# The order behind the state steps of a two-layer hybrid trunk, its last residual sum on two engines, and one weight split behind an eviction

## The chip, the cores and the metric

The kernel runs on one core of a Trainium2 chip. The core has TensorE for matrix products, VectorE, ScalarE and GpSimd for work on elements, and SyncE (SP), which here only issues transfers. Every engine works through a queue of its own, in order, and waits on semaphores that the others raise. The metric is the device time of one execution in microseconds, lower is better.

## What is computed

A trunk of two layers on 256 tokens of width 1024, float32. Each layer is, cut to what matters here:

```
u = rms_norm(x)
q, k, v, z, a, b, cq, ckv, k_rope, gates = split(u @ W_in)
# branch A: short causal conv and SiLU on q, k, v; l2 norm of q and k; gated delta rule in chunks
o_a = gated_delta_rule(q, k, v, g, beta)          # per head, a triangular solve and a state step
y_a = (rms_norm(o_a) * silu(z)) @ W_a
# branch B: latent attention with rotary keys
q_b = rms_norm(cq) @ W_uq ; k_b, v_b = rms_norm(ckv) @ W_ukv ; k_pe = rope(k_rope)
y_b = softmax(q_b k_b^T + mask) v_b @ W_b
h = sigmoid(g_A) * y_a + sigmoid(g_B) * y_b ;  x = x + rms_norm(h @ W_out)
x = x + rms_norm(relu(rms_norm(x) @ W1)^2 @ W2)
```

## The kernel before

Everything is held transposed, features on the 128 partitions and the 256 tokens along the free dimension, so a tile of two feature chunks is 128x512. A dense product is made of three products of split operands: each operand is a high part (`whi`, `uh`, `xh`) in a short format and a low part (`wlo`, `ul`, `xl`), and TensorE computes hi x hi, lo x hi and hi x lo into one of three PSUM banks `dense`. The weights come as 152 pieces a layer of 128x1024 through a ring of four buffers: SP loads `raw`, ScalarE copies it to `whi` (`split_hi`), VectorE subtracts to get `wlo` (`split_lo`), TensorE uses both. SP may load a piece when the `wlo` of the piece four before is made; ScalarE may write `whi` when TensorE is through with the piece four before.

One list, `ORDER`, is written out by the function `schedule`, and each engine walks it once per layer and takes from each entry what is its own. So `ORDER` sets the queue of every engine. An entry `("job", j)` is a dense product of 256 output features with its eviction, `("half", j)` the first half of one. Ahead of an entry stand the splits of the pieces that `splits_wanted` gives it: a job asks for the splits up to four pieces ahead of its last one. The kinds of job are: `lat` (the latents; the third, `lat` 2, also holds the rotary key and the logits a and b, which VectorE puts into `krx`), `k`, `z`, `v`, `q`, `gate`, `kn` and `vt` (keys and values of branch B), `uq` (its queries), `ya`, `yb`, `out`, `ff1` and `ff2`.

The small steps that the text speaks of are entries too. `t_v0`, `t_st`, `t_ks` and `t_v1` are the state steps of the delta rule between its two chunks, with VectorE's `vn` and `rr`; `qk` is the product of keys and queries (L888) with VectorE's decay of it into `DT` (L1667); `t_o` forms the output `oT` from 24 small products (L1009 to L1011), and ScalarE evicts it. `q2` is a square of `qT` on ScalarE (L1270), which enters the norm of the output. That norm has for each of four pairs of heads: `osq`, ScalarE's square of `oT` (L1276) and GpSimd's addition of `q2` to it (L1914), into one of two buffers `sq`; `onrm`, TensorE's sum over the partitions (L1020), ScalarE's logarithm and exponential (L1120, L1122) and VectorE's scaling of `oT` (L1718); `osplit`, GpSimd's product with `zs` (L1920) and the split into `oh` and `ol`. `osq` of pair 2 or 3 waits until the sum of the pair two before has left the buffer. `kr` is the rotary turn of the shared key: one product (L856) and VectorE's block of seven operations from `krb` to `krz`; `qrope` is the same for the queries. `lnexp` loads a table of functions on ScalarE. `sc`, `tr` and `pv` are the attention: scores, the softmax on VectorE (L1733 to L1743), transposes (L1056), values. `logits` starts with a product of `krx` (L787).

At the end of a layer `post` scales `yT` by `rn` (`times_norm`, L1810) and adds it to `xT` (`add`, L1815) on VectorE; in the last layer SP stores `xT` in four pairs of chunks as they come.

Of the kernel before, what the change touches and what calls it, by code (L numbers as in the profile page):

```python
# [19 lines left out]
ALU = mybir.AluOpType  # L20
# [4 lines left out]
DEPTH, D, S = 2, 1024, 256  # L25
# [18 lines left out]
RING = 4  # L44
# [42 lines left out]
JOBS, NPIECE = jobs_of_a_layer()  # L87
JOB = {(kind, i): j for j, (kind, i, _) in enumerate(JOBS)}
# [4 lines left out]
NDVE_EVAC = NJOB - NACT_EVAC  # L93
# [17 lines left out]
def evacs_through(j):  # L111

    mine = JOBS[j][0] in EVAC_BY_ACT
    return mine, sum((k in EVAC_BY_ACT) == mine for k, _, _ in JOBS[:j + 1])
# [5 lines left out]
def schedule():  # L120
# [4 lines left out]
    def job(kind, i, after=None):  # L125
        o.append(("job", JOB[kind, i]))
        flush()
        if after:
            late.append((after, i))
# [47 lines left out]
    behind = {n: [] for n in range(len(shares))}  # L177
# [8 lines left out]
    behind[3].append(("trig", 0))  # L186
    for n, at_ in enumerate((7, 9, 10, 13)):
        behind[at_].insert(0, ("vtrans", n))
    for n, at_ in enumerate((1, 3)):
        behind[at_].insert(0, ("ktrans", n))  # L190
    steps = [[(step, lv)] for lv in range(len(SIZES)) for step in ("lvP", "lvV")]
# [3 lines left out]
    for n, share in enumerate(shares):  # L195
# [11 lines left out]
            o.extend(ready[at_unit])  # L207
            at_unit += 1
        o.extend(behind[n])
    o.append(("q2", 0))  # L210
    job("vt", 0)
    o += [("qk", 0), ("qk", 1), ("qd", 0), ("kr", 0)]
    job("vt", 1)
    o += [("q2", 1), ("q2", 2), ("q2", 3), ("lnexp", 1), ("t_o", 0)]
    job("vt", 2)
    o += [("qk", 2), ("qk", 3), ("qd", 1)]
    job("vt", 3)
    for n, i in enumerate((4, 5, 0, 1, 2, 3)):
        job("uq", i)
        if i >= 4:  # L220
            late.append(("qrope", i - 4))
        if n == 0:
            o.append(("t_o", 1))
        if n >= 2:
            o.append(("onrm", n - 2))
        if 1 <= n < 5:
            o.append(("osq", n - 1))
    o += [("exptanh", 0), ("sc", 0), ("osplit", 0), ("osplit", 1)]
    for n in range(6):
        job("gate", 1 + n)  # L230
# [47 lines left out]
def build(nc, x_in, pos_in, w_in, prm_in, cst_in, out):  # L278
    with ExitStack() as ctx:
# [17 lines left out]
        xT = keep("xT", [P, KD, S])  # L297
# [107 lines left out]
        def over_heads(ap, n):  # L405

            return ap.rearrange("p (a w) -> p a w", a=1).broadcast_to([P, n, ap.shape[1]])
# [84 lines left out]
        def due(l, s, n):  # L492

            return l * rises_per_layer[s.name] + n
# [24 lines left out]

        def splits_wanted(l, what, n):  # L520

            if what == "job":
                return min(l * NPIECE + JOBS[n][2][-1] + RING, DEPTH * NPIECE)
            if what == "half":
                return l * NPIECE + JOBS[n][2][0] + RING
            if what == "ahead":
                return min(l * NPIECE + (NPIECE if n else JOBS[JOB["ff1", 0]][2][0]) + RING, DEPTH * NPIECE)
            if what == "u":
                return l * NPIECE + (8 if n >= 2 else 0)
            if l:  # L530
                return l * NPIECE + (4 if (what, n) == ("xsplit", 1) else 0)
            return {("xsplit", 1): 1, ("xsplit", 2): 2, ("sq", 0): 3, ("sqsum", 1): 4}.get((what, n), 0)
# [13 lines left out]
        @block.sync  # L546
        def _(sp):
            def x_part(c):
                sp.dma_start(xT[:, 2 * c:2 * c + 2, :], x_in[:, 2 * c:2 * c + 2, :]).then_inc(s_x[c], 16)

            for n in range(DEPTH * NPIECE):
                if n == 2:
                    x_part(2)
                    x_part(3)
                elif n < 2:
                    x_part(n)
                sp.wait_ge(lo_ready, n + 1)
                sp.dma_start(raw[n % RING][:], w_in[n]).then_inc(loaded[n % RING], 16)
                if n == RING - 1:
                    sp.dma_start(cst[:, 0:C_FREQ], cst_in[:, 0:C_FREQ]).then_inc(s_in, 16)  # L560
                    sp.dma_start(pos_i[:], pos_in).then_inc(s_tab, 16)
                    sp.dma_start(cst[:, C_FREQ:NCST], cst_in[:, C_FREQ:NCST]).then_inc(s_tab, 16)
            for c in range(4):
                pair = slice(2 * c, 2 * c + 2)
                sp.wait_ge(x_done, due(DEPTH, x_done, 2 * c + 2))
                sp.dma_start(out[:, pair, :], xT[:, pair, :]).then_inc(s_out, 16)
            sp.wait_ge(s_out, 4 * 16)

# [862 lines left out]
        def _(dve):  # L1431
# [373 lines left out]
            def post(l, n):  # L1805
                w, part = divmod(n, 2)

                def times_norm(c0, c1):
                    cs = slice(c0, c1)
                    TT(yT[:, cs, :], yT[:, cs, :], over_heads(rn[0][:, 0:S], c1 - c0), ALU.mult).then_inc(y_scaled, c1 - c0)  # L1810
# [6 lines left out]
                def low(e):  # L1817
# [6 lines left out]
                    elif l + 1 < DEPTH:  # L1824
                        x_low(l + 1, e)

                if part:
                    low(6)
                    low(7)
                    return  # L1830
                dve.wait_ge(y_r, due(l, y_r, 2 * w + 2))
                dve.wait_ge(dve_evac, l * NDVE_EVAC + evacs_through(JOB["ff2" if w else "out", 3])[1])
                times_norm(0, 1)
                add(0, 1)
                times_norm(1, 2)
# [39 lines left out]
        def _(pool):  # L1875
# [47 lines left out]
                pool.wait_ge(dve_evac, l * NDVE_EVAC + evacs_through(JOB["ff1", i])[1])  # L1923
                G(fr[i % 4][:], fr[i % 4][:], fr[i % 4][:], ALU.mult).then_inc(f_sq, 1)  # L1924

            do = dict(squares=squares, yadd=yadd, qd=qd_, zero=zero, osq=osq, osplit=osplit, fsplit=fsplit)
            pool.wait_ge(s_in, 16)
            for l in range(DEPTH):
                for what, n in ORDER:
# [115 lines left out]
```

## Time and profile before

| | us |
|---|---|
| median of 3 runs | 1043.33 (1041.62 to 1043.66) |
| profiled execution | 1044.15 |
| its span | 1042.4 |
| TensorE busy | 1013.2 (97%) |
| VectorE busy | 727.2 (70%) |
| ScalarE busy | 559.0 (54%) |
| GpSimd busy | 96.4 (9%) |

The span runs from the first to the last instruction of one execution; the profiled execution took 1.75 us more. Busy shares are of the span. The granted clock of TensorE was 0.993 of full speed over the span. In the names of the profile PE is TensorE, DVE is VectorE, ACT is ScalarE, POOL is GpSimd, and SPq is SP's queue of transfers; L1020 is line 1020 of the kernel.

### The profile page before, as it was taken

How to read it: one execution, taken by the hardware profiler on the slowest of the kernel's cores; microseconds unless marked ns; L12 is line 12 of the kernel's file. 1: busy time of each engine (PE TensorE's matmuls, PEld its weight loads, DVE VectorE, ACT ScalarE, POOL GpSimd, SP SyncE). 2: the span in 40 equal slices, each digit the busy share in tenths (PEclk: the TensorE clock that was granted, in tenths of full speed). 3: DMA queues.
4: the chain of work that ended last, by engine and by line, in shares of the span. 5: the costliest groups of instructions: out<-in, count | busy, mean ns of one | idle time of the engine just before them, and what ended most of it. 6: DMA issues, size and time to landing. Idle time of an engine off the chain costs nothing.

```text
span 1042.4 us, 24322 instructions
## 1 busy us (share of the span) xinstructions
PE 1013.2 (97%) x10626; PEld 984.9 (94%) x10626; DVE 727.2 (70%) x1024; ACT 559.0 (54%) x791; POOL 96.4 (9%) x76
## 2 busy tenths in 40 slices
PE   9999999899999999999999999998999999999996
PEld 8999899799999999999999999997999999999995
DVE  7887766588566788644598667656865777885543
ACT  7665684645445645444466645756554445544441
POOL 0010000120000222100000100004000003221000
PEclk9999999999999999999999989999999999999998
DMA  8544433424565466666635344333255646666661
GB/s 294 163 130 136 145 105 120 120 75 169 177 190 181 135 200 193 202 198 188 181 105 179 122 127 146 119 104 120 84 180 182 186 139 190 195 191 198 198 182 41
DMA packets 45609, 163.86 MB, mean 157 GB/s; under 512 B 5184, under 2 KB 5440, under 8 KB 45504
## 3 DMA queue, kind: packets, MB, share of 16 engines
q1 hardware_dynamic: 45360, 162.16, 50.2%
q8 instruction: 84, 1.38, 0.5%
q14 instruction: 21, 0.17, 0.1%
q10 hardware_dynamic: 144, 0.15, 0.0%
HBM read 161.25 MB, written 1.05 MB: 156 GB/s over the span
## 4 chain that ended last, share of the span: by engine, by line
PE 82%; issue 8%; DVE 7%; ACT 2%; POOL 1%; DMA 0%; SPq 0%; DVEq 0%; POOLq 0%; ACTq 0%
PE dense L613 22%; PE dense L614 21%; PE dense L615 21%; DVE wlo L1450 2%; POOL sq L1914 1%; PE sides L1070 1%; PE sides L1044 1%; PE sides L1045 1%; PE sides L918 1%; PE dense L596 1%; PE dense L598 1%; PE dense L597 1%; PE sides L598 1%; PE sides L597 1%; PE sides L596 1%
## 5 line engine op out<-in xcount | busy, mean ns | idle before, releaser
L1450 DVE TENSOR_TENSOR wlo<-raw,whi 128x1024 fp32r<-128x1024 f32 (+1 forms) x303 | 390.1, 1295 | 201.9 <-ACT whi L1105 201.4
L1105 ACT ACTIVATE whi<-raw 128x1024 fp32r<-128x1024 f32 (+2 forms) x305 | 315.7, 1044 | 214.4 <-PE dense L615 193.7
L613 PE MATMUL dense<-uh,whi 128*128 128x256 f32 x768 | 222.6, 290 | 4.2 <-issue 2.6
L614 PE MATMUL dense<-ul,whi 128*128 128x256 f32 x768 | 215.0, 280 | 0.1
L615 PE MATMUL dense<-uh,wlo 128*128 128x256 f32 x768 | 214.9, 280 | 0.0
L613 PEld LDWEIGHTS dense<-uh,whi 128*128 128x128 f32 x768 | 146.4, 191 | 6.0 <-issue 2.1
L614 PEld LDWEIGHTS dense<-ul,whi 128*128 128x128 f32 x768 | 145.9, 190 | 2.0 <-issue 1.7
L615 PEld LDWEIGHTS dense<-uh,wlo 128*128 128x128 f32 x768 | 145.7, 190 | 0.2 <-issue 0.2
L613 PE MATMUL dense<-fuh,whi 128*128 128x256 f32 x512 | 142.5, 278 | 0.4 <-DVE ful L1822 0.4
L614 PE MATMUL dense<-ful,whi 128*128 128x256 f32 x512 | 141.5, 276 | 0.0
L615 PE MATMUL dense<-fuh,wlo 128*128 128x256 f32 x512 | 141.5, 276 | 0.0
L613 PE MATMUL dense<-fh,whi 128*128 128x256 f32 x384 | 106.0, 276 | 0.0
L614 PE MATMUL dense<-fl,whi 128*128 128x256 f32 x384 | 106.0, 276 | 0.0
L615 PE MATMUL dense<-fh,wlo 128*128 128x256 f32 x384 | 106.0, 276 | 0.0
L613 PEld LDWEIGHTS dense<-fuh,whi 128*128 128x128 f32 x512 | 96.1, 188 | 1.6 <-issue 1.1
L614 PEld LDWEIGHTS dense<-ful,whi 128*128 128x128 f32 x512 | 96.3, 188 | 0.1
L615 PEld LDWEIGHTS dense<-fuh,wlo 128*128 128x128 f32 x512 | 96.1, 188 | 0.0
L613 PEld LDWEIGHTS dense<-fh,whi 128*128 128x128 f32 x384 | 72.1, 188 | 0.0
L614 PEld LDWEIGHTS dense<-fl,whi 128*128 128x128 f32 x384 | 72.1, 188 | 0.0
L615 PEld LDWEIGHTS dense<-fh,wlo 128*128 128x128 f32 x384 | 72.1, 188 | 0.0
L1924 POOL TENSOR_TENSOR fr<-fr 128x512 f32<-128x512 f32 x32 | 44.9, 1405 | 117.5 <-DVE fr L1791 117.5
L1894 POOL TENSOR_TENSOR sq<-sq,sq 128x512 f32<-128x512 f32 x8 | 10.4, 1299 | 349.2 <-ACT sq L1241 349.2
(320 smaller groups left out, 2079.7 us busy)
## 6 DMA issues: line engine op xcount, KB each, us to landing
raw<-weights SPq DMA_DIRECT2D x304, 512.0 KB, 3.8
xT<-x_t SPq DMA_DIRECT2D x4, 256.0 KB, 5.5
out_t<-xT SPq DMA_DIRECT2D x4, 256.0 KB, 2.3
cst<-consts SPq DMA_DIRECT2D x1, 512.0 KB, 8.3
prm_all<-params ACTq DMA_DIRECT2D x1, 150.0 KB, 4.0
pos_i<-pos SPq DMA_DIRECT2D x1, 128.0 KB, 7.9
cst<-consts SPq DMA_DIRECT2D x1, 6.0 KB, 7.8
```

Source lines behind the costliest of these rows:

```text
L596: mm(o_, h_[:, ws], ahi[:, k0 + k, :], start=first and k == 0, stop=False, skip_group_check=True)
L597: mm(o_, h_[:, ws], alo[:, k0 + k, :], start=False, stop=False, skip_group_check=True)
L598: x_ = mm(o_, l_[:, ws], ahi[:, k0 + k, :], start=False, stop=last and k == 3, skip_group_check=True)
L613: mm(o_, h_[:, ws], ahi[:, k0 + k, :], start=is_first, stop=False, skip_group_check=True)
L614: mm(o_, h_[:, ws], alo[:, k0 + k, :], start=False, stop=False, skip_group_check=True)
L615: x_ = mm(o_, l_[:, ws], ahi[:, k0 + k, :], start=False, stop=is_last, skip_group_check=True)
L918: r = mm(side[e][rows, 16 * g:16 * (g + 1)], XTq[rows, e, g, :], PBq[rows, e, g, 0:16], start=True, stop=True)
L1044: mm(o_, qn[:, h, qt * P:(qt + 1) * P], kn[:, h, 0:w], start=True, stop=False)
L1045: r = mm(o_, qr[:, h // 2, qt * P:(qt + 1) * P], krz[:, h % 2, 0:w], start=False, stop=True)
L1105: return A(o_, i_, ACT.Copy)
L1450: TT(wlo[s][:, 0:w], raw[s][:, 0:w], f32(whi[s][:, 0:w]), ALU.subtract).then_inc(lo_ready, 1)
L1924: G(fr[i % 4][:], fr[i % 4][:], fr[i % 4][:], ALU.mult).then_inc(f_sq, 1)
```

## The change

Three things are changed. In `schedule`, behind the state step `t_ks`, the entries between the `kn` jobs and the last `uq` job are put in another order: `q2` and `kr` come ahead of `t_v1`, the `qk` entries ahead of the `vt` jobs, `t_o` between them, and `osq` and `onrm` each earlier. In `splits_wanted` the third latent job asks for one split less, which then comes with the next entry. In the last layer, `post` on VectorE handles six of the eight chunks, in operations of two chunks, and a new `post` of GpSimd the last two; SP waits for GpSimd's semaphore ahead of the fourth store.

```
--- before.py
+++ after.py
@@ -186,6 +186,7 @@
     behind[3].append(("trig", 0))
     for n, at_ in enumerate((7, 9, 10, 13)):
         behind[at_].insert(0, ("vtrans", n))
+    behind[14] += [("q2", 0), ("q2", 1), ("kr", 0)]
     for n, at_ in enumerate((1, 3)):
         behind[at_].insert(0, ("ktrans", n))
     steps = [[(step, lv)] for lv in range(len(SIZES)) for step in ("lvP", "lvV")]
@@ -207,24 +208,23 @@
             o.extend(ready[at_unit])
             at_unit += 1
         o.extend(behind[n])
-    o.append(("q2", 0))
+    o += [("q2", 2), ("q2", 3), ("lnexp", 1), ("qk", 0), ("qk", 1), ("qd", 0)]
     job("vt", 0)
-    o += [("qk", 0), ("qk", 1), ("qd", 0), ("kr", 0)]
+    o += [("qk", 2), ("qk", 3), ("qd", 1)]
     job("vt", 1)
-    o += [("q2", 1), ("q2", 2), ("q2", 3), ("lnexp", 1), ("t_o", 0)]
+    o.append(("t_o", 0))
     job("vt", 2)
-    o += [("qk", 2), ("qk", 3), ("qd", 1)]
+    o += [("t_o", 1), ("osq", 0)]
     job("vt", 3)
+    o.append(("osq", 1))
     for n, i in enumerate((4, 5, 0, 1, 2, 3)):
         job("uq", i)
         if i >= 4:
             late.append(("qrope", i - 4))
-        if n == 0:
-            o.append(("t_o", 1))
-        if n >= 2:
-            o.append(("onrm", n - 2))
-        if 1 <= n < 5:
-            o.append(("osq", n - 1))
+        if 1 <= n <= 4:
+            o.append(("onrm", n - 1))
+        if 1 <= n <= 2:
+            o.append(("osq", n + 1))
     o += [("exptanh", 0), ("sc", 0), ("osplit", 0), ("osplit", 1)]
     for n in range(6):
         job("gate", 1 + n)
@@ -519,6 +519,8 @@
 
         def splits_wanted(l, what, n):
 
+            if what == "job" and JOBS[n][:2] == ("lat", 2):
+                return l * NPIECE + JOBS[n][2][0] + RING
             if what == "job":
                 return min(l * NPIECE + JOBS[n][2][-1] + RING, DEPTH * NPIECE)
             if what == "half":
@@ -562,7 +564,10 @@
                     sp.dma_start(cst[:, C_FREQ:NCST], cst_in[:, C_FREQ:NCST]).then_inc(s_tab, 16)
             for c in range(4):
                 pair = slice(2 * c, 2 * c + 2)
-                sp.wait_ge(x_done, due(DEPTH, x_done, 2 * c + 2))
+                if c == 3:
+                    sp.wait_ge(y_add, due(DEPTH, y_add, 2))
+                else:
+                    sp.wait_ge(x_done, due(DEPTH, x_done, 2 * c + 2))
                 sp.dma_start(out[:, pair, :], xT[:, pair, :]).then_inc(s_out, 16)
             sp.wait_ge(s_out, 4 * 16)
 
@@ -1824,12 +1829,22 @@
                     elif l + 1 < DEPTH:
                         x_low(l + 1, e)
 
+                if part and w and l + 1 == DEPTH:
+                    return
                 if part:
                     low(6)
                     low(7)
                     return
                 dve.wait_ge(y_r, due(l, y_r, 2 * w + 2))
                 dve.wait_ge(dve_evac, l * NDVE_EVAC + evacs_through(JOB["ff2" if w else "out", 3])[1])
+                if w and l + 1 == DEPTH:
+                    times_norm(0, 2)
+                    times_norm(2, 4)
+                    add(0, 2)
+                    times_norm(4, 6)
+                    add(2, 4)
+                    add(4, 6)
+                    return
                 times_norm(0, 1)
                 add(0, 1)
                 times_norm(1, 2)
@@ -1923,7 +1938,17 @@
                 pool.wait_ge(dve_evac, l * NDVE_EVAC + evacs_through(JOB["ff1", i])[1])
                 G(fr[i % 4][:], fr[i % 4][:], fr[i % 4][:], ALU.mult).then_inc(f_sq, 1)
 
-            do = dict(squares=squares, yadd=yadd, qd=qd_, zero=zero, osq=osq, osplit=osplit, fsplit=fsplit)
+            def post(l, n):
+
+                if n != 2 or l + 1 < DEPTH:
+                    return
+                pool.wait_ge(y_r, due(l, y_r, 4))
+                pool.wait_ge(dve_evac, l * NDVE_EVAC + evacs_through(JOB["ff2", 3])[1])
+                G(yT[:, 6:8, :], yT[:, 6:8, :], over_heads(rn[0][:, 0:S], 2), ALU.mult).then_inc(y_add, 1)
+                pool.wait_ge(y_add, due(DEPTH, y_add, 1))
+                G(xT[:, 6:8, :], xT[:, 6:8, :], yT[:, 6:8, :], ALU.add).then_inc(y_add, 1)
+
+            do = dict(post=post, squares=squares, yadd=yadd, qd=qd_, zero=zero, osq=osq, osplit=osplit, fsplit=fsplit)
             pool.wait_ge(s_in, 16)
             for l in range(DEPTH):
                 for what, n in ORDER:
```

ScalarE's queue in layer 0 at the `uq` jobs, before: `sq` from `oT` is `osq`, `qr` and `qn` are evictions of `uq` jobs, the two rows on `rn` are `onrm`, `whi` is a weight split.

```order
L1105 ACTIVATE qr<-dense 128x512
L1276 ACTIVATE sq_66<-oT 128x512
L1105 ACTIVATE whi_55<-raw_51 128x768
L1105 ACTIVATE qn<-dense 128x512
L1120 ACTIVATE rn_68<-sides,bias_cols 128x512
L1122 ACTIVATE rn_68<-rn_68 128x512
L1276 ACTIVATE sq_67<-oT 128x512
L1105 ACTIVATE whi_56<-raw_52 128x1024
L1105 ACTIVATE qn<-dense 128x512
L1120 ACTIVATE rn_69<-sides,bias_cols 128x512
L1122 ACTIVATE rn_69<-rn_69 128x512
L1276 ACTIVATE sq_66<-oT 128x512
```

The same place now:

```order
L1281 ACTIVATE sq_66<-oT 128x512
L1110 ACTIVATE vt<-dense 128x512
L1281 ACTIVATE sq_67<-oT 128x512
L1110 ACTIVATE whi_57<-raw_53 128x768
L1110 ACTIVATE qr<-dense 128x512
L1110 ACTIVATE whi_54<-raw_50 128x768
L1110 ACTIVATE qr<-dense 128x512
L1125 ACTIVATE rn_68<-sides,bias_cols 128x512
L1127 ACTIVATE rn_68<-rn_68 128x512
L1281 ACTIVATE sq_66<-oT 128x512
L1110 ACTIVATE whi_55<-raw_51 128x768
L1110 ACTIVATE qn<-dense 128x512
```

Both buffers `sq_66` and `sq_67` are now written ahead of the first `uq` eviction, and the third square stands directly behind the first norm.

VectorE's queue in layer 0 at the third latent job, before: `latT` and `krx` are its eviction, `wlo` a weight split, `ul` the low part of the normed input.

```order
L1479 TENSOR_TENSOR ul<-utmp,uh 128x512
L1450 TENSOR_TENSOR wlo_58<-raw_50,whi_54 128x1024
L1767 TENSOR_SCALAR latT<-dense,prm_all 128x256
L1771 TENSOR_TENSOR krx<-dense,rn_69 80x256
L1450 TENSOR_TENSOR wlo_59<-raw_51,whi_55 128x1024
L1450 TENSOR_TENSOR wlo_60<-raw_52,whi_56 128x1024
```

The same place now:

```order
L1484 TENSOR_TENSOR ul<-utmp,uh 128x512
L1772 TENSOR_SCALAR latT<-dense,prm_all 128x256
L1776 TENSOR_TENSOR krx<-dense,rn_69 80x256
L1455 TENSOR_TENSOR wlo_58<-raw_50,whi_54 128x1024
L1455 TENSOR_TENSOR wlo_59<-raw_51,whi_55 128x1024
L1455 TENSOR_TENSOR wlo_60<-raw_52,whi_56 128x1024
```

The split into `wlo_58` has moved from ahead of `latT` to behind `krx`; on ScalarE the split into `whi_54` moves in the same way behind the square of the same job.

VectorE's queue at the end of the last layer, before:

```order
L1778 TENSOR_SCALAR yT<-dense,prm_all 128x256
L1778 TENSOR_SCALAR yT<-sides,prm_all 128x256
L1810 TENSOR_TENSOR yT<-yT,rn_68 128x256
L1815 TENSOR_TENSOR xT<-xT,yT 128x256
L1810 TENSOR_TENSOR yT<-yT,rn_68 128x256
L1815 TENSOR_TENSOR xT<-xT,yT 128x256
L1810 TENSOR_TENSOR yT<-yT,rn_68 128x512
L1815 TENSOR_TENSOR xT<-xT,yT 128x512
L1810 TENSOR_TENSOR yT<-yT,rn_68 128x512
L1815 TENSOR_TENSOR xT<-xT,yT 128x512
L1810 TENSOR_TENSOR yT<-yT,rn_68 128x512
L1815 TENSOR_TENSOR xT<-xT,yT 128x512
```

VectorE's queue there now:

```order
L1783 TENSOR_SCALAR yT<-sides,prm_all 128x256
L1815 TENSOR_TENSOR yT<-yT,rn_68 128x512 x2
L1820 TENSOR_TENSOR xT<-xT,yT 128x512
L1815 TENSOR_TENSOR yT<-yT,rn_68 128x512
L1820 TENSOR_TENSOR xT<-xT,yT 128x512 x2
```

GpSimd's queue at the same place now, where before its last row was the addition into `sq_66`:

```order
L1939 TENSOR_TENSOR fr_143<-fr_143 128x512
L1939 TENSOR_TENSOR fr_144<-fr_144 128x512
L1909 TENSOR_TENSOR sq_66<-sq_66,sq_67 128x512 x2
L1947 TENSOR_TENSOR yT<-yT,rn_68 128x512
L1949 TENSOR_TENSOR xT<-xT,yT 128x512
```

VectorE's ten operations of `post` have become six of full width, and GpSimd has two that it did not have.

## Rows read from the trace of the kernel before

**Rows 1.** The page, part 1: busy us (share of the span) xinstructions.

```profile
PE 1013.2 (97%) x10626; PEld 984.9 (94%) x10626; DVE 727.2 (70%) x1024; ACT 559.0 (54%) x791; POOL 96.4 (9%) x76
```

**Rows 2.** Who waited for whom, TensorE: us in total, times, longest us.

```profile
PE sides L1020 <- POOL sq L1914: 8.5, 6, 1.7
...
PE sides L787 <- DVE krx L1771: 1.0, 2, 0.5
```

**Rows 3.** Rows in time, TensorE: start us, us, engine, line, tiles [idle before].

```profile
172.08 0.39 PE L742 MATMUL dense<-whi,lath 128*128 128x512 f32 x1
...
173.45 1.95 PE L888 MATMUL sides<-qT,kT 128*128 128x128 f32 x16
...
204.51 1.13 PE L1020 MATMUL sides<-sq,cst 128*128 128x512 f32 x2 [1.29 <-POOL sq L1914]
...
208.99 1.13 PE L1020 MATMUL sides<-sq,cst 128*128 128x512 f32 x2 [1.29 <-POOL sq L1914]
...
218.99 0.60 PE L1056 MATMUL sides<-cst,E 128*128 128x128 f32 x4
```

**Rows 4.** Rows in time, ScalarE, layer 0.

```profile
181.20 1.28 ACT L1285 ACT_TABLE_LOAD   x1
...
205.67 0.69 ACT L1120 ACTIVATE rn<-sides,bias_cols 128x512 f32<-128x512 f32 x1 [1.18 <-PE sides L1020]
206.39 0.63 ACT L1122 ACTIVATE rn<-rn 128x512 f32<-128x512 f32 x1
206.93 0.61 ACT L1276 ACTIVATE sq<-oT 128x512 f32<-128x512 f32 x1
207.45 1.04 ACT L1105 ACTIVATE whi<-raw 128x1024 fp32r<-128x1024 f32 x1
```

**Rows 5.** Rows in time, GpSimd, layer 0 (208.89 alone, then all four).

```profile
192.83 1.29 POOL L1914 TENSOR_TENSOR sq<-sq,q 128x512 f32<-128x512 f32 x1 [27.49 <-ACT sq L1276]
...
208.89 2.25 POOL L1920 TENSOR_TENSOR oT<-oT,zs 128x512 f32<-128x512 f32 x1
...
208.89 6.44 POOL L1920 TENSOR_TENSOR oT<-oT,zs 128x512 f32<-128x512 f32 x4
```

**Rows 6.** Rows in time, VectorE, layer 0.

```profile
168.65 0.69 DVE L1705 TENSOR_TENSOR vn<-sides,sm 128x512 f32<-128x512 f32 x1 [0.30 <-PE sides L999]
...
176.23 0.41 DVE L1623 TENSOR_TENSOR krb<-sides,sinT 64x256 f32<-64x256 f32 x1
...
177.64 0.81 DVE L1629 TENSOR_TENSOR krz<-krb,kra 64x256 f32<-64x256 f32 x2
...
193.10 1.57 DVE L1636 TENSOR_TENSOR qr<-qr,cosT 128x512 f32<-128x512 f32 x1
...
208.52 1.49 DVE L1450 TENSOR_TENSOR wlo<-raw,whi 128x1024 fp32r<-128x1024 f32 x1 [0.72 <-ACT whi L1105]
...
217.51 0.69 DVE L1743 TENSOR_TENSOR E<-E,rs 128x512 f32<-128x512 f32 x1
```

**Rows 7.** Rows in time, all engines, behind the third latent job.

```profile
30.16 0.37 ACT L1219 ACTIVATE sq_q<-dense 128x256 f32<-128x256 f32 x1
...
30.28 1.23 DVE L1450 TENSOR_TENSOR wlo<-raw,whi 128x1024 fp32r<-128x1024 f32 x1 [0.18 <-ACT whi L1105]
...
31.82 0.41 DVE L1771 TENSOR_TENSOR krx<-dense,rn 80x256 f32<-80x256 f32 x1
...
32.29 0.28 PE L787 MATMUL sides<-cst,krx 16*128 16x16 f32 x1 [0.50 <-DVE krx L1771]
```

**Rows 8.** Rows in time, all engines, the end.

```profile
1033.63 0.42 DVE L1810 TENSOR_TENSOR yT<-yT,rn 128x256 f32<-128x256 f32 x1 [1.23 <-ACT rn L1122]
...
1035.22 0.69 DVE L1810 TENSOR_TENSOR yT<-yT,rn 128x512 f32<-128x512 f32 x1
1035.33 4.61 SPq L566 DMA_DIRECT2D out_t<-xT  x4
...
1038.89 0.69 DVE L1815 TENSOR_TENSOR xT<-xT,yT 128x512 f32<-128x512 f32 x1
```

## The prediction

> **What bounds the kernel now.** I read the busy shares first. TensorE is busy for 1013.2 of 1042.4 us [rows 1], so a change can pay only where TensorE stands still, some 29 us: about 10 us behind its last product, 19 us in waits. The list of who waited for whom says which waits. The largest is the sum of squares of the output norm, L1020 (`onrm`), which waited 8.5 us in 6 waits for GpSimd's addition; the small product of `logits`, L787, waited 1.0 us in 2 [rows 2]. TensorE's rows show that these six waits repeat: L1020 starts at 204.51 and again at 208.99, each time after 1.29 us of standing still, so the loop turns in 4.48 us [rows 3]. ScalarE's and GpSimd's rows give the ring. L1020 is through at about 205.64; ScalarE then takes the logarithm (205.67) and the exponential (206.39), and only behind them in its own queue stands the next square (206.93 to 207.54); GpSimd's addition takes 1.29; TensorE starts at 208.99 [rows 3 to 5]. TensorE's own work in a turn (one `uq` job and one L1020) is 4.48 - 1.29 = 3.2 us. The wait is thus one of order: the square is issued one entry before it is needed.
>
> **The evidence on the new order of `onrm` and `osq`.** The change puts the first two squares ahead of the `uq` jobs, and square n+2 behind norm n. Between L1020 number 0 and number 2 TensorE now has `uq` 0, a `qrope` product, L1020 number 1 and `uq` 1: at 3.2 us a turn over 6 us, with the `qrope` product more. What must happen meanwhile is 0.7 + 0.6 + 0.6 us on ScalarE and 1.3 us on GpSimd, 3.3 us with the gaps of the ring [rows 4, 5]. The ring has about 3 us to spare, and all six waits should go: 6 waits, **-8.5 us**. ScalarE must carry it: per turn a split (1.0), an eviction (0.5, as the square beside it), two norm activations (1.3) and at times a square (0.5) [rows 4], 2.8 to 3.3 us, against TensorE's 3.2, or 4.1 where there is a `qrope` product; the square stands in just these longer turns.
>
> **What pays for it, ahead of it.** No instruction of this part is added or removed; they move.
> - `kr` comes ahead of `t_v1`. On VectorE it is a block from 176.23 to 178.45, 2.2 us [rows 6], and behind it now wait the two `vn` of `t_v1`, for which the first `qk` product waits. Worked out: VectorE is free at 168.65 - 0.30 = 168.35, ends `kr` at 170.6 and the two `vn` (0.6 each) at 171.9. TensorE comes to `qk` at 173.45 now; one `vt` job (172.08 to 173.45) moves behind and the `kr` product (0.6) ahead, so at about 172.65 [rows 3]. The slack is 0.7 us, and I price this at 0. With no slack it would be at most 1 us a layer.
> - On ScalarE four `q2` squares (0.5 each) and the table load of 1.28 us [rows 4] now all stand ahead of the first `vt` eviction. I follow the queue: they end at about 175.1, the split of piece 45 at 175.9, the first `vt` product at 175.8. Before, this eviction waited for `kr` until 178.5, so it comes earlier, not later. The splits of pieces 46 and 47 end at about 183.6 and 189.3; TensorE asks for them at about 193 and 197. Price 0, covered by 7 us of other products. The weight transfers queued on SP follow these splits: the load of piece 51 waits for `wlo` of 47, 190.3 instead of 187.4, lands 4 us later, and its split is due at 201.6. Free.
> - The `qk` and `t_o` products only change places between `vt` jobs.
>
> **What comes behind.** GpSimd's four `osplit` products, 6.44 us in a row [rows 5], ran after the last norm; now they run between the norms and meet VectorE. The rows say that the two engines shut each other out on operands in SBUF: `qr` at 193.10 took 1.57 us instead of about 0.69, ending 0.55 us after GpSimd's addition (192.83 + 1.29 = 194.12); GpSimd's first `osplit` took 2.25 us, 1.13 after VectorE's split (208.52 + 1.49 = 210.01) was through [rows 5, 6]. Counting every such turn, VectorE finishes its last `oT` norm near 207.7 and the next split near 208.8; the softmax row ending in L1743 is ready at about 213.1 where it was at 218.20, 5.1 us earlier [rows 6]. TensorE's transposes (218.99) would come 4.3 us earlier, at 214.7 [rows 3]. The slack grows from 0.8 to 1.6 us, so the 4.26 us per layer pass on. If VectorE were to lose more than 1.6 us there, the rest would come back as a wait before L1056.
>
> **The third latent job.** ScalarE's square (30.16) and VectorE's `latT` and `krx` (to 32.23) stand behind the split of the piece that `z` needs (30.28 to 31.51), and TensorE waits 0.50 us for `krx` [rows 7]. With the split behind them, `krx` ends near 30.8, a microsecond before TensorE's 31.79. The split then ends near 32.0; TensorE asks for that piece right behind L787, at 32.3. Slack 0.3 us. So -0.5 us, twice: **-1.0 us**. Should the split come 0.3 us later than I think, half of it is lost.
>
> **The end.** Before, VectorE alone ran ten operations from 1033.63 to 1039.58, SP's last transfer was issued until 1035.33 + 4.61 = 1039.94, and the span ended at 1042.4 [rows 8]. Now VectorE has six of 128x512 (0.69, spaced 0.61), GpSimd two, and SP's fourth transfer stands behind the third. With the exclusion above, from 1033.63: VectorE to 1034.32, GpSimd 1.13 to 1035.45, VectorE 0.55 to 1036.00, GpSimd to 1037.13, VectorE 0.55 to 1037.68, then three of 0.61: 1039.51. That is 0.07 us earlier, but the fourth transfer is issued 0.36 us behind the third, where now it is the last: **+0.3 us**. Bounds: with no exclusion VectorE ends at 1033.63 + 0.69 + 5 x 0.61 = 1037.4, so -2.2 + 0.36 = -1.8 us; with GpSimd at 6.44 / 4 = 1.6 us an operation and the last transfer held up by the one ahead (0.4, my estimate) +1.7 us. I take the value by the exclusion, since its two rows are of the same operations.
>
> The Trainium skill speaks against this part: "SBUF — State Buffer", section "SBUF: two separate sides", calls the port pair of VectorE and GpSimd an exclusive lock, held for a whole instruction, when a VectorE operation has two SBUF inputs. The 1.57 and 2.25 us above agree with it; by the rule the end is worth +0.3, without it -1.8. The Trainium skill's page "Perfetto Trace Analysis", section "GPSIMD Engine Instruction", also says to time GpSimd by the spacing of starts and not by its spans; the spacing is the 1.6 us of the upper bound, by which the end would be +1.3 instead of +0.3.
>
> **Sum.** -8.5 - 1.0 + 0.3 = -9.2 us. The profiled execution took 1044.15 us (span 1042.4 and 1.75 around it) and would take 1034.9; it was 0.8 above the median of 1043.33. From the median: **1034.1 us**.
>
> **The rivals.**
> 1. The end gains, because the engines overlap there: -1.8 in place of +0.3, 1032.0 us. For it: GpSimd reads a broadcast operand, which no row shows. Against: the rows of the exclusion. 0.10.
> 2. The crowding of VectorE and GpSimd, or `kr` ahead of `t_v1`, gives part back: 1 us before `qk` and 1 to 2 us before L1056 per layer, 4 us in all, 1038 us. For it: slacks of 0.7 and 1.6 us, worked out over a dozen turns. 0.15.
> 3. The loop keeps its waits, because ScalarE is the ring: if its turn is 4.4 us instead of 3.3 the six waits stay, and only `logits` gains, 1042.5 us. Against: its rows sum to 3.3. 0.03.
> 4. Slower: GpSimd's eight operations per layer at 1.28 us each land wholly on VectorE's path to the softmax, 10.2 us per layer. It decides above 1.6 + 4.3 + 0.5 = 6.4 us per layer; at 10.2 the time is 1043.3 + 2 x 3.8 + 0.3, about 1051 us. Against: before, four of the eight stood on that path as well, with 0.8 us of slack left. 0.02.
>
> The forecast has 0.70. The range must hold 0.8: it reaches over rival 1 and most of rival 2, to 1031.5 and 1037.8; the spread of the three runs (2 us) lies inside. About 0.2% (2 us) is what a measurement of this kernel can tell from no change. Faster: forecast, rivals 1 and 2, 0.95. Same: rival 3 mostly, 0.03. Slower: 0.02.
>
> **What would show it.** In the profile of the changed kernel: L1025 (the same line, moved by 5) with no wait for GpSimd; no wait of TensorE's `qk` for `vn`; the table load ahead of the first `vt` eviction; L792 without its 0.5 us; `osplit` of GpSimd between the norms, with VectorE operations of 1.4 us and more beside it; the softmax ready ahead of the transposes; in the end two `yT` of VectorE with a stretched second one and GpSimd's last result near 3.5 us after the start. Wrong if new waits of TensorE of over 1 us stand before `qk`, before the transposes, or before a `dense` product for `wlo`; or if VectorE's six last operations take less than 4.5 us.

## The result, and the profile after

The changed kernel takes **1032.18 us**, the median of 4 runs (1030.74 to 1032.70), where the kernel before took 1043.49 on the same chip (4 runs, 1041.62 to 1045.19). The ratio is 0.989, with a 95% interval of 0.987 to 0.9909. That is 11.3 us less by the medians; the forecast was 1034.1 in a range of 1031.5 to 1037.8. The profiled execution took 1032.70 us with a span of 1030.9, 11.5 below the span before.

The page's first part, busy us (share of the span) xinstructions:

```profile
PE 1011.5 (98%) x10626; PEld 985.0 (96%) x10626; DVE 730.6 (71%) x1020; ACT 558.7 (54%) x791; POOL 102.5 (10%) x78
```

TensorE's busy time fell by only 1.7 us [rows 1], so 9.8 of the 11.5 us are time in which it had stood still. The list of its waits says which (here without its smallest row). Columns: engine, tile, line, waited for: us in total, times, longest us.

```profile
PE sides L915 <- issue: 2.7, 2, 2.2
PE dense L618 <- issue: 1.9, 1, 1.9
PE sides L581 <- DVE sq L1875: 1.6, 1, 1.6
PE dense L618 <- DVE ul L1484: 1.4, 3, 0.5
PE dense L618 <- DVE ful L1827: 0.4, 2, 0.2
PE dense L618 <- DVE wlo L1455: 0.3, 1, 0.3
```

L1025 (L1020 before) and L792 (L787 before) are gone from it [rows 2], and no wait has come in their place. TensorE's rows in layer 0 (start us, us, engine, line, tiles, [idle before]) answer to [rows 3]:

```profile
172.31 1.95 PE L893 MATMUL sides<-qT,kT 128*128 128x128 f32 x16
...
191.75 1.02 PE L1025 MATMUL sides<-sq,cst 128*128 128x512 f32 x2
...
195.52 1.02 PE L1025 MATMUL sides<-sq,cst 128*128 128x512 f32 x2
...
198.44 1.02 PE L1025 MATMUL sides<-sq,cst 128*128 128x512 f32 x2
...
201.42 1.02 PE L1025 MATMUL sides<-sq,cst 128*128 128x512 f32 x2
...
213.62 0.60 PE L1061 MATMUL sides<-cst,E 128*128 128x128 f32 x4
```

A turn of the loop is now 198.44 to 201.42, 2.98 us, where it was 4.48; the turn ahead of it takes 2.92. Nothing stands in brackets behind the four pairs: they wait for nobody.

GpSimd's and VectorE's rows of the same stretch answer to [rows 5, 6]. First GpSimd:

```profile
194.76 1.32 POOL L1929 TENSOR_TENSOR sq<-sq,q 128x512 f32<-128x512 f32 x1 [4.95 <-ACT sq L1281]
198.53 1.43 POOL L1929 TENSOR_TENSOR sq<-sq,q 128x512 f32<-128x512 f32 x1 [2.45 <-ACT sq L1281]
199.92 3.98 POOL L1935 TENSOR_TENSOR oT<-oT,zs 128x512 f32<-128x512 f32 x2
204.53 2.19 POOL L1935 TENSOR_TENSOR oT<-oT,zs 128x512 f32<-128x512 f32 x1 [0.63 <-DVE oT L1723]
207.36 2.21 POOL L1935 TENSOR_TENSOR oT<-oT,zs 128x512 f32<-128x512 f32 x1 [0.63 <-DVE oT L1723]
```

And VectorE:

```profile
170.09 1.29 DVE L1710 TENSOR_TENSOR vn<-sides,sm 128x512 f32<-128x512 f32 x2
...
198.74 1.77 DVE L1723 SCALAR_TENSOR_TENSOR oT<-oT,prm_all,rn 128x512 f32<-128x512 f32 x1
...
205.51 1.77 DVE L1723 SCALAR_TENSOR_TENSOR oT<-oT,prm_all,rn 128x512 f32<-128x512 f32 x1
207.20 1.21 DVE L1455 TENSOR_TENSOR wlo<-raw,whi 128x1024 fp32r<-128x1024 f32 x1
...
212.10 0.69 DVE L1748 TENSOR_TENSOR E<-E,rs 128x512 f32<-128x512 f32 x1
```

The addition of 194.76 is over at 196.08 and its norm comes at 198.44: 2.4 us of slack where there was a wait. The next addition, of 198.53, is over at 199.96 and its norm comes at 201.42: here the slack is 1.5 us. The price is to be seen as well: `osplit` now runs between the norms, and VectorE's norms that meet an operation of GpSimd take 1.77 us, the one of 198.74 beside the addition, the one of 205.51 beside an `osplit`.

At the third latent job (all engines, answering to [rows 7]):

```profile
29.29 0.36 ACT L1224 ACTIVATE sq_q<-dense 128x256 f32<-128x256 f32 x1
...
30.49 0.41 DVE L1776 TENSOR_TENSOR krx<-dense,rn 80x256 f32<-80x256 f32 x1
30.82 3.48 DVE L1455 TENSOR_TENSOR wlo<-raw,whi 128x1024 fp32r<-128x1024 f32 x3
31.81 0.61 PE L792 MATMUL sides<-cst,krx 16*128 16x16 f32 x4
```

`krx` is ready at 30.90, 0.9 us ahead of L792, and the moved split runs behind it.

The end, answering to [rows 8]:

```profile
1021.33 1.26 POOL L1947 TENSOR_TENSOR yT<-yT,rn 128x512 f32<-128x512 f32 x1 [22.84 <-ACT rn L1127]
1021.34 3.46 DVE L1815 TENSOR_TENSOR yT<-yT,rn 128x512 f32<-128x512 f32 x2 [1.28 <-ACT rn L1127]
1022.67 1.59 POOL L1949 TENSOR_TENSOR xT<-xT,yT 128x512 f32<-128x512 f32 x1
1024.73 0.68 DVE L1820 TENSOR_TENSOR xT<-xT,yT 128x512 f32<-128x512 f32 x1
1025.33 0.68 DVE L1815 TENSOR_TENSOR yT<-yT,rn 128x512 f32<-128x512 f32 x1
1025.43 2.64 SPq L571 DMA_DIRECT2D out_t<-xT  x4
1025.93 1.28 DVE L1820 TENSOR_TENSOR xT<-xT,yT 128x512 f32<-128x512 f32 x2
```

VectorE needs 1027.21 - 1021.34 = 5.87 us for six operations; its first two alone take 3.46. GpSimd is through at 1024.26, yet its result is stored last. From the start of the scaling to the end of the span are 1030.9 - 1021.34 = 9.56 us, where they were 1042.4 - 1033.63 = 8.77: **this part is a loss of 0.8 us**.

**Where the time came from.** I set the starts of the same TensorE rows beside each other, after minus before. From the `st` products of L992 to the rows behind the softmax (L1070) the difference goes from -0.64 to -5.57 in layer 0 and from -7.52 to -12.64 in layer 1: 4.93 and 5.12, together **-10.05 us** for the new order. From the last `dense` product ahead of each of the two `logits` products to the `logits` product itself (31.51 to 32.29 before, 31.60 to 31.81 now) it moves by -0.57 and again -0.57, **-1.15**. The end gives **+0.8**. The remaining 1.1 us lie in stretches that the change leaves alone: issue stalls of TensorE, that is, standstills for which the profile shows no wait, and the clock behind them. The largest single step, 1.2 us, lies behind such a stall (1.74 us before, at 612.52, and 2.17 us now, at 606.74).

### The profile page after: what moved, and what is told of

It is laid out like the page before. It is cut to its first block, busy times and chain, and to the rows that moved or that the text cites. A ratio compares the mean times of both kernels' runs of the same rounds, so it can differ in the third digit from the quotient of the medians.

```text
span 1030.9 us, 24316 instructions
## 1 busy us (share of the span) xinstructions
PE 1011.5 (98%) x10626; PEld 985.0 (96%) x10626; DVE 730.6 (71%) x1020; ACT 558.7 (54%) x791; POOL 102.5 (10%) x78
## 4 chain that ended last, share of the span: by engine, by line
PE 89%; DVE 7%; ACT 2%; issue 2%; DMA 0%; DVEq 0%; SPq 0%; ACTq 0%
PE dense L618 23%; PE dense L620 22%; PE dense L619 22%; DVE wlo L1455 2%; PE sides L1075 1%; PE sides L1049 1%; PE sides L1050 1%; PE sides L923 1%; PE dense L601 1%; PE dense L603 1%; PE sides L603 1%; PE sides L601 1%; PE dense L602 1%; PE sides L602 1%; PE sides L915 1%
## 5 line engine op out<-in xcount | busy, mean ns | idle before, releaser
L1909 POOL TENSOR_TENSOR sq<-sq,sq 128x512 f32<-128x512 f32 x8 | 10.4, 1299 | 349.9 <-ACT sq L1246 349.9
```

The lines of the kernel that those rows point to most:

```text
L1909: G(sq[0][:], sq[0][:], sq[1][:], ALU.add).then_inc(y_add, 1)
```

## The experiments

My theory is that the gain is the ring of ScalarE's queue, opened by the order of `osq` and `onrm` in the `uq` loop, and that the end pays for the split over two engines. Its rivals: the gain comes from what moved ahead of the loop (`kr`, `q2`, `qk`); or the end gains and the rest less than it seems. Each experiment was timed beside the kernel before on the same chip; all differences below are against the before of its own group.

### One part at a time

Four kernels. `e1_order_alone` has the change's edit of `schedule` and nothing else; its core:

```diff
+        if 1 <= n <= 4:
+            o.append(("onrm", n - 1))
+        if 1 <= n <= 2:
+            o.append(("osq", n + 1))
```

> The new order alone, without the latent job's split and without the split end. Theory of the ring: all six waits before L1020 go, and each was worth about 1.5 to 1.6 us (the turn falls from 4.48 us to about 2.95) rather than the 1.4 that the profile lists as idle, because the product behind a wait also starts from an emptied pipeline: -9.5 to -10 us against before. Rival, the listed idle time is all there is: -8.5 us, and the rest of the change's 11.3 us comes from the other two parts or from TensorE's stalls of issue lying elsewhere.

`e2_latent_alone` has the two lines of `splits_wanted` alone:

```diff
+            if what == "job" and JOBS[n][:2] == ("lat", 2):
+                return l * NPIECE + JOBS[n][2][0] + RING
```

> Only the split of the third latent job moved. My term: -0.5 us a layer, -1.0 in all, the wait of TensorE for krx (0.50 us, twice) gone. Rival: about 0.9 us a layer, -1.7, since in the changed kernel TensorE gained another 0.36 us between this product and the next of the gate sums in both layers; if that belongs to this edit it shows here too. Second rival: nothing, since VectorE's later split holds TensorE up.

`e3_end_alone` has the new `post` of VectorE and GpSimd and SP's wait alone; `e4_end_undone` is the changed kernel without them:

```diff
-                if c == 3:
-                    sp.wait_ge(y_add, due(DEPTH, y_add, 2))
-                else:
-                    sp.wait_ge(x_done, due(DEPTH, x_done, 2 * c + 2))
+                sp.wait_ge(x_done, due(DEPTH, x_done, 2 * c + 2))
```

> Only the split end of the last layer. Theory of exclusion: VectorE ends 5.9 us behind its start as before, and the last store is issued and lands later: +0.8 us from the scaling's start to the end of the span (9.56 against 8.77 us). Rival, the two engines overlap: -1.8 us.

> The changed kernel with the end of before. Theory of exclusion: 0.8 us faster than the changed kernel, so -12.1 us against before (1031.4 by the medians). Rival, overlap of the engines pays: 1 to 2 us slower than the changed kernel.

Against a before of 1042.43 us (23 runs):

| kernel | median us (runs) | ratio [95%] |
|---|---|---|
| e1, order alone | 1032.75 (5) | 0.9912 [0.9897, 0.9927] |
| e2, latent alone | 1041.62 (12) | 0.9993 [0.9981, 1.0005] |
| e3, end alone | 1043.39 (12) | 1.0012 [1.0001, 1.0023] |
| e4, order and latent | 1031.91 (6) | 0.9902 [0.9885, 0.9919] |

The order alone makes 9.7 of the 11.3 us. Its two regions gain 4.93 and 5.21 us, as in the changed kernel, and of the two waits that the change aims at only the one for `krx` is left in its list. The latent part alone is too small for the run times: its interval holds 1. The trace shows it. In e2's list of TensorE's waits L789, which is L787 moved by two lines, no longer stands, its rows gain 0.58 and 0.56 us there, and the large one is whole:

```profile
PE sides L1022 <- POOL sq L1916: 8.4, 6, 1.7
```

The end alone is slower, by an interval that just leaves out 1: +0.96 us by the medians, and 9.54 us from the scaling's start to the end of its span, as in the changed kernel. Without it, e4 needs 8.7 for this stretch. By the medians e4 and the changed kernel can't be told apart (1031.91 and 1032.18, measured beside different runs); the stretch tells them apart by 0.86 us.

### The loop alone

`e9_loop_alone` is the kernel before with the new rule inside the `uq` loop only; `kr`, `q2`, `qk` and `vt` stay where they were.

```diff
         if n == 0:
-            o.append(("t_o", 1))
-        if n >= 2:
-            o.append(("onrm", n - 2))
-        if 1 <= n < 5:
-            o.append(("osq", n - 1))
+            o += [("t_o", 1), ("osq", 0), ("osq", 1)]
+        if 1 <= n <= 4:
+            o.append(("onrm", n - 1))
+        if 1 <= n <= 2:
+            o.append(("osq", n + 1))
```

> Of the new order only the loop: the first two osq directly behind the second t_o, onrm and the last two osq one entry earlier; q2, kr, qk, the vt jobs and t_o stay where they were. If the ring is all that the new order breaks, this alone gives nearly all of it: the six waits before L1020 gone, -9.5 to -10 us against before. Rival, the parts moved ahead of it are needed, because else the first two squares come too late: a wait before the first or second L1020 of 1 to 2 us a layer, so only -6 to -8 us.

It takes 1034.36 us (5 runs) beside 1042.84 (9 runs): ratio 0.9917 [0.99, 0.9934], 8.5 us by the medians. In its trace all six waits before L1020 are gone from the list, and its regions gain 4.63 and 4.82 us, 9.45 of the order's 10.05. The rival that the steps ahead of the loop bring the gain falls: they bring 0.3 to 0.4 us a layer. Where that lies is to be seen. GpSimd's first addition now starts at 192.31, where in the changed kernel it starts at 187.28, and the first L1020 comes a little late for it: from the start of the L1028 pair ahead to its own are 1.15 us (192.48 to 193.63), in the changed kernel 0.86 (190.89 to 191.75). It is the wait that the rival named, at 0.3 us in place of 1 to 2.

### Doubling the suspected wait

In both kernels GpSimd does its addition in `osq` twice, the first time into a scratch buffer that nobody reads. If the addition is on the ring, the kernel before pays for it in every turn; in the changed kernel there should be room.

```diff
+                G(PT[i % 2][:], sq[i % 2][:], q2[:, pair, :].rearrange("p c s -> p (c s)"), ALU.add)
```

The edit's other two lines, a wait of GpSimd for its own addition two pairs before, are left out here.

> The kernel before with GpSimd's addition of osq done twice, first into a buffer that nothing reads (about 1.3 us more in each of the four). The ring predicts that each of the three waits of a layer grows by 1.3 us: +7.8 us in all, 1050.2. Rival, the waits before L1020 come from ScalarE's queue or from the shape of the product: less than 2 us.

> The same doubling in the changed kernel. With about 3 us to spare between a square and its sum nothing waits before L1025: 0 to 0.5 us there. What GpSimd holds VectorE up may show before the transposes, where the softmax is now 0.8 us ahead: up to 1.5 us a layer, so 0 to +3 us in all. Rival, the new order only just fits: +7.8 us as before.

Before, so doubled, takes 1059.39 us (4 runs) beside 1042.60 (10 runs): ratio 1.0172 [1.0145, 1.02], 16.8 us slower, twice what I expected. Its list of waits has:

```profile
PE sides L1020 <- POOL sq L1917: 17.8, 8, 3.5
```

The wait grew by 9.3 us, near the 7.8 expected; two of its eight places are new, 0.42 us each, before the first L1020 of a layer. Much of the other 7.5 us comes by another way, which its windows of layer 0 show (window, us, PE busy (x), PEld, DVE, ACT, POOL, TensorE's granted clock, DMA share, GB/s):

```profile
198.00:201.00 3.00, 0.08 (x1) 0.00 (x0) 3.00 (x3) 1.37 (x2) 2.98 (x2) 0.85 0.34 134
201.00:204.00 3.00, 2.95 (x8) 1.92 (x9) 1.08 (x1) 0.81 (x2) 0.00 (x0) 0.50 0.26 97
204.00:207.00 3.00, 2.96 (x14) 2.67 (x13) 1.74 (x2) 1.98 (x3) 1.89 (x2) 0.51 0.20 78
207.00:209.00 2.00, 0.29 (x1) 0.29 (x2) 0.53 (x1) 0.60 (x1) 1.65 (x1) 1.00 0.37 51
```

TensorE stood still for 2.96 us ahead of 201.05, and for the 6 us behind it the granted clock is 0.50, the 1.2 GHz level: 8 and 14 products in 3 us where the window of 209 to 212, at the full 2.4 GHz level, has 20. The L1020 pair behind that wait takes 2.08 us, the later ones of this layer 1.12:

```profile
201.05 2.08 PE L1020 MATMUL sides<-sq,cst 128*128 128x512 f32 x2 [2.96 <-POOL sq L1917]
...
208.71 1.12 PE L1020 MATMUL sides<-sq,cst 128*128 128x512 f32 x2 [1.74 <-POOL sq L1917]
...
215.40 1.12 PE L1020 MATMUL sides<-sq,cst 128*128 128x512 f32 x2 [3.51 <-POOL sq L1917]
```

In layer 1 two of the pairs take 1.97 and 2.08 us in the same way. It is not the wait's length alone: the pair at 215.40, behind 3.51 us, takes 1.12. Equal rows give the sizes. From L992 to L1070 this kernel loses 7.56 and 8.02 us in its two layers, 15.6 in all, of which the longer waits are 9.3. The granted clock is 0.50 while TensorE works from 201.05 to 206.9, from 722.3 to 725.7 and from 729.75 to 732.6, some 12 us; at the full level that work would take half, so the clock is worth about 6 us, an estimate from these rows. The two together give 15.3 of the 15.6.

The changed kernel, doubled in the same way, takes 1033.90 us (5 runs), ratio 0.9933 [0.991, 0.9956]: 1.7 us above the median of the changed kernel. That one was measured beside another before; each against its own, this kernel gains 8.7 us and the changed kernel 11.3, so 2.6 less. Its rows say 3.3 less: the two regions gain 3.28 and 3.50 us, where it was 4.93 and 5.12. No wait before L1025 stands in its list; the room that the order made took the second addition up, and just so: the last one of layer 0 is over at 202.49, and its norm starts at 202.55, after a turn of 3.18 us in place of 2.98. The new row is another:

```profile
PE sides L1061 <- DVE E L1748: 2.1, 2, 1.2
```

It is the place that the prediction named for the crowding of VectorE and GpSimd, and it says how much room is left there: about 1.3 us more of GpSimd's work for each of four pairs, partly beside VectorE's, used up the 0.8 us of slack and 1 us more in each layer. So the same extra work costs 15.6 us of TensorE's rows in the one order and 3.3 in the other (16.8 and 1.7 to 2.6 by the medians).

### The end, in three forms

`e5_end_interleaved` leaves all eight operations with VectorE, at full width and with each addition a step behind its scaling, and nothing with GpSimd:

```diff
                 if w and l + 1 == DEPTH:
                     times_norm(0, 2)
                     times_norm(2, 4)
                     add(0, 2)
                     times_norm(4, 6)
                     add(2, 4)
+                    times_norm(6, 8)
                     add(4, 6)
+                    add(6, 8)
```

> The new order and the moved split, and the end on VectorE alone: eight operations of two chunks in the interleaved order, none on GpSimd, the stores as before. If the split end is held back by the exclusion of the two engines and by its late last store, this end takes 0.69 + 7 x 0.61 = 5.0 us on VectorE instead of 5.9, and from the scaling's start to the end of the span 7.8 us instead of 9.6: 1.8 us faster than the changed kernel. Rival, VectorE's chain was never what held the end: no more than 0.5 us.

`e6_store_order` is the changed kernel with GpSimd's chunks, ready first, stored first:

```diff
-            for c in range(4):
+            for c in (3, 0, 1, 2):
```

> The changed kernel with GpSimd's pair stored first, not last. GpSimd's result is there 3 us before VectorE's last. If the last store's place behind the third costs 0.4 us of issue and 0.4 us of landing, both go: 0.8 us from the span, 9.56 to about 8.8 us. Rival, the landing is longer for another reason: only 0.4 us.

`e11_end_no_reads` takes the operands away from GpSimd:

```diff
-                G(yT[:, 6:8, :], yT[:, 6:8, :], over_heads(rn[0][:, 0:S], 2), ALU.mult).then_inc(y_add, 1)
+                nc.gpsimd.memset(yT[:, 6:8, :], 0.0).then_inc(y_add, 1)
-                G(xT[:, 6:8, :], xT[:, 6:8, :], yT[:, 6:8, :], ALU.add).then_inc(y_add, 1)
+                nc.gpsimd.memset(xT[:, 6:8, :], 0.0).then_inc(y_add, 1)
```

> The changed kernel, where GpSimd's two operations of the end are fills with zero that read nothing, so the last two chunks of the result are not computed. If what holds VectorE up is that both read operands from SBUF, VectorE's six operations now take 0.69 + 5 x 0.61 = 3.7 us instead of 5.9, with none of them stretched. Rival, any work of GpSimd's on SBUF holds it up: above 5 us.

`e5` has the lowest median of all the correct kernels: **1029.75 us** (5 runs, 1029.31 to 1031.82) beside 1042.60, ratio 0.9888 [0.9869, 0.9907]. Its end:

```profile
1020.12 1.29 DVE L1812 TENSOR_TENSOR yT<-yT,rn 128x512 f32<-128x512 f32 x2 [1.28 <-ACT rn L1124]
1021.33 0.68 DVE L1817 TENSOR_TENSOR xT<-xT,yT 128x512 f32<-128x512 f32 x1
...
1022.04 3.34 SPq L568 DMA_DIRECT2D out_t<-xT  x4
...
1023.74 1.28 DVE L1817 TENSOR_TENSOR xT<-xT,yT 128x512 f32<-128x512 f32 x2
```

VectorE alone does eight operations in 1025.02 - 1020.12 = 4.90 us, where together with GpSimd it took 5.87 for six. The end is 7.88 us, 1.7 shorter than the changed kernel's. The whole medians differ by 2.4 us in the same direction, 1.5 with each against its own before, and the intervals of the two ratios overlap almost wholly: it is the stretch that tells the two apart.

`e6` takes 1031.04 us (5 runs, ratio 0.9897 [0.9879, 0.9916]), and its stretch is 1029.2 - 1020.50 = 8.70 us, 0.86 shorter than the changed kernel's. SP's first issue now stands at 1023.44, while VectorE is still at work; the last one has nothing ahead of it:

```profile
1023.44 3.29 SPq L571 DMA_DIRECT2D out_t<-xT  x4
```

`e11` leaves the last two chunks of the result uncomputed and shows the exclusion by itself. One run took 1029.37 us:

```profile
1020.14 0.53 POOL L1947 MEMSET yT<- 128x512 f32 x1 [22.82 <-ACT rn L1127]
1020.17 1.29 DVE L1815 TENSOR_TENSOR yT<-yT,rn 128x512 f32<-128x512 f32 x2 [1.28 <-ACT rn L1127]
...
1022.59 1.28 DVE L1820 TENSOR_TENSOR xT<-xT,yT 128x512 f32<-128x512 f32 x2
```

The same six operations of VectorE now take 1023.87 - 1020.17 = 3.70 us instead of 5.87, and the first two 1.29 instead of 3.46, although GpSimd still writes to the same places at the same time. GpSimd's operations are shorter here, 0.53 us for 1.26 and 1.59, but nothing of VectorE's beside them is stretched at all. It is GpSimd's reading of SBUF, the on-chip memory that holds these tiles, that shuts VectorE out. The Trainium skill, "SBUF — State Buffer", section "SBUF: two separate sides", says the same: a VectorE operation with two SBUF inputs takes the lock only against a GpSimd operation that reads SBUF. This run agrees.

### How far the same program repeats itself

`e10_before_again` is the kernel before, unchanged, profiled once more.

> The kernel before, unchanged, profiled once more. If TensorE's stalls of issue (5.1 us in the first profile) and the pace of its products differ from execution to execution, their sum or their places differ here by 1 to 2 us, the waits before L1020 stay at 8.5 us and the one before L787 at 1.0. Rival, they belong to the program: the same stalls in the same places.

It took 1041.96 us with a span of 1040.2. The named waits are the same; the issue stalls are not:

```profile
PE sides L1020 <- POOL sq L1914: 8.4, 6, 1.7
PE sides L910 <- issue: 3.0, 2, 2.2
...
PE sides L787 <- DVE krx L1771: 0.9, 2, 0.5
```

Beside the first profile its rows are 2.2 us late near 103 us, even again (within 0.3) at 128 us, and 2.3 us early at 620 us. So one and the same program moves by 2.2 us from one execution to the next, and it does so where TensorE stood still for "issue". The windows at the last of these places, first profile and then this one, show that most of it is the granted clock, 0.86 of full speed against 1.00:

```profile
600.00:625.00 25.00, 23.26 (x527) 22.65 (x526) 16.43 (x27) 12.31 (x17) 0.00 (x0) 0.86 0.41 130
600.00:625.00 25.00, 22.84 (x665) 22.03 (x664) 17.86 (x30) 13.68 (x22) 0.00 (x0) 1.00 0.46 147
```

The changed kernel has 0.93 there. This movement is larger than the 1.1 us that my three parts leave over.

## Why the prediction was right, and which terms were off

**The loop, -8.5.** Right in place and mechanism: all six waits went, and e9 and e7 show that they were the ring of `osq` and `onrm`. The size was short: the term is worth 10.05 us. A listed wait counts only the idle time. The turn went from 4.48 to 2.98 us, 1.5, where 1.29 had stood idle. The other 0.2 us lies on both sides of the wait. Behind it, the L1020 pair takes 1.13 us [rows 3] and 1.02 without a wait. Ahead of it, the last product is shown busy for 0.28 us, while products that follow one another start 0.12 us apart: from its start to that of L1020 are 1.57 us before (202.94 to 204.51) and 0.12 now (201.30 to 201.42), 1.45 us where the list has 1.29. The first wait of a layer was longer, 1.67 us [rows 2: longest 1.7], which lifts the mean to 1.7. I took 3.2 us for TensorE's own work in a turn; it is 2.92 to 2.98. And the 3 us that I gave the ring to spare are 2.4 for the third pair and 1.5 for the fourth; e8's second addition fills the latter.

**What moved ahead of the loop, 0.** Right: no wait came of it. The trace's rows here are 0.64 us early against before, so each needs that added. `vn` is ready at 171.38 and `qk` starts at 172.31, a slack of 0.9 us where I had 0.7. The splits of pieces 46 and 47 end at 183.3 and 188.9 (I had 183.6 and 189.3). The table load ends at 175.4, with the 0.64 a microsecond later than worked out, with no wait for it.

**The crowding, 0.** Right, by less room than I thought. VectorE's last norm ends at 207.28 and its next split at 208.41; with the 0.64 added, 207.9 and 209.0 against my 207.7 and 208.8. The softmax is ready at 212.79 (213.4; I had 213.1), and TensorE asks at 213.62 (214.3; I had 214.7), since it is faster in the loop than I had it. The slack is 0.83 us, not 1.6. Rival 2 was nearer than I had priced it, and e8 shows the wait that it spoke of, once GpSimd has more to do.

**The third latent job, -1.0.** Measured -1.15, and -1.14 in e2; a listed wait of 0.50 us is worth 0.57 here too. The moved split ends about 0.3 us ahead of TensorE, as said.

**The end, +0.3.** Measured +0.8, inside the bounds. The step was right for the engines: 5.88 us worked out, 5.87 measured, by two durations under the exclusion (1.13 and 0.55). GpSimd won the first turn and was through at 2.9 us, not near 3.5, which changes nothing for VectorE. What I mis-sized is the last store. I counted its issue, 0.36 us, and had the other 0.4 us only in the upper bound: SP's last issue ends 6.7 us after the scaling's start (6.3 before), and SP then waits 2.4 us for it to land, where it waited 2.0. e6, which changes nothing but the order of the stores, gives 0.86 us back, the whole of this loss. The Trainium skill's rule in "Perfetto Trace Analysis", section "GPSIMD Engine Instruction", to go by the spacing of GpSimd's starts, would have given the end another microsecond with the spacing of 1.6 us that I had from the kernel before; in these rows the durations of single operations gave the sum, and the measurement decides.

**The whole.** The sum was -9.2 us; the three parts measure -10.4. The loop was 1.55 us short, and the end, off by 0.5 the other way, hid part of that. The last 1.1 us of the spans' difference is not in the change, as far as the traces tell: it lies in stretches whose instructions are the same, and e10 moves by more with no change at all. That no small effect of the change is in it I can't show. The time alone would have misled: 1032.18 lies 0.2 us from rival 1's 1032.0 and 1.9 from the forecast, though the end, on which rival 1 rests, lost time. Only the stretches tell the two apart.

Rival 1 (the end gains) is out by e3, e4 and e11; rival 3 (the loop keeps its waits) by e1 and e9; rival 4 (slower) needed 6.4 us a layer, and the crowding cost nothing.

## What to carry to other kernels

Where one engine waits for a small operation again and again with the same idle time, write down the ring with each engine's queue in it: here ScalarE's square stood behind an exponential that it did not need, and issuing it one entry earlier, without one instruction less, took 1% off the kernel. A list of idle times understates such a wait, here 1.4 us each for 1.7. At a kernel's end don't split SBUF-to-SBUF work over VectorE and GpSimd: VectorE alone, at full width and with the dependent operations interleaved, was 1 us faster; and let no finished store queue behind one that is still waited for.

## What the hardware showed that I had not expected

- TensorE's granted clock fell to the 1.2 GHz level behind a standstill of 2.96 us and stayed there for 6 us (e7), while in the kernel before it is 1.00 in every window of the loop, behind waits of 1.3 to 1.7 us, and in e7 a wait of 3.51 us had no lower clock behind it. Stalls for "issue" go with it too, and not by their length: near 612 us the kernel before stood still for 1.74 us and had the lower level (0.86 over the window above), while the same program in e10 stood still for 2.17 us and had 1.00. Why it falls in the one and not in the other no run here shows. In the changed kernel a stall of 1.89 us at 99.22, where before had 0.94, was followed by the lower level. The changed kernel's window behind that stall:

```profile
99.20:102.00 2.80, 2.79 (x14) 2.79 (x15) 2.20 (x4) 0.90 (x2) 0.00 (x0) 0.58 0.17 66
```

and the same window of the kernel before:

```profile
99.20:102.00 2.80, 2.80 (x26) 2.80 (x27) 2.80 (x6) 0.10 (x1) 0.00 (x0) 1.00 0.38 146
```

14 products against 26 in the same 2.8 us: here the changed kernel is 1.8 us behind the other for a while. So a wait can cost more behind it than its own length.
- VectorE and GpSimd take strict turns when both read SBUF: each waits out the other's whole operation. Two scalings of VectorE take 3.46 us with GpSimd's two operations beside them and 1.29 without; the second of them ends at 1024.80, 0.54 us behind GpSimd's last at 1024.26.
